# A mixture-of-experts block on one Trainium2 core: w_down products with the tokens as stationary operand in every item, the slots beyond 128 on four column groups

## The reference

```python
logits = h2 @ w_router + b_router            # h2 = rms_norm(x, g_ffn), 32 experts
top_vals, top_idx = top_k(logits, 4)
gates = softmax(top_vals)
for each expert e and each token that chose it:
    a = h2[token] @ w_up[e] + b_up[e]                     # 1024 -> 2048
    hidden = min(a_glu, 7) * sigmoid(1.702 * min(a_glu, 7)) * (clip(a_lin, -7, 7) + 1)
    x[token] += gate * (hidden @ w_down[e] + b_down[e])   # 1024 -> 1024
out = rms_norm(x, g_final)
```

## Time and profile before

| | us |
|---|---|
| median of 3 runs | 2034.45 (2033.26 to 2040.49) |
| the profiled execution, its own time | 2039.02 |
| its span in the trace | 2037.3 |
| TensorE busy in the span | 1969.0 (97%) |
| VectorE, ScalarE, GpSimd busy | 771.6, 653.8, 202.2 |
| mean granted clock of TensorE | 0.983 of full speed |

### The profile page before, as it was taken

The page is one execution under the profiler, slowest core; times in us unless marked ns, Lnnn a source line. Parts: engine busy times, 40 slices in busy tenths (PEclk is TensorE's granted clock), DMA queues, the critical chain, the costliest instruction groups (busy, mean ns, idle before and its releaser), DMA issues.

```text
span 2037.3 us, 38850 instructions
## 1 busy us (share of the span) xinstructions
PE 1969.0 (97%) x14762; PEld 1837.5 (90%) x14762; DVE 771.6 (38%) x1908; ACT 653.8 (32%) x1093; POOL 202.2 (10%) x210
## 2 busy tenths in 40 slices
PE   6999999998699999999999999999999999999997
PEld 5677788877689999999999999999999999999997
DVE  4343277423455445544555442222222222222114
ACT  4222255322155455544555441111111111111113
POOL 0000000001111111111111111111111111110010
PEclk9999899999799999999999999999999999999999
DMA  5223844132799899989998998888888777777774
GB/s 187 79 78 130 255 103 109 55 104 93 260 379 336 310 328 337 332 310 330 339 338 307 332 326 291 287 286 276 288 285 272 269 264 249 259 255 246 259 243 189
DMA packets 241871, 508.02 MB, mean 249 GB/s; under 512 B 13703, under 2 KB 14343, under 8 KB 241792
## 3 DMA queue, kind: packets, MB, share of 16 engines
q1 hardware_dynamic: 224704, 457.91, 63.8%
q0 software_dynamic: 16000, 47.31, 8.2%
q10 hardware_dynamic: 1120, 2.16, 0.3%
HBM read 469.55 MB, written 46.33 MB: 253 GB/s over the span
## 4 chain that ended last, share of the span: by engine, by line
PE 77%; DMA 1%; DVE 1%; issue 1%; ACT 1%; SPq 0%; POOL 0%; DVEq 0%; ACTq 0%; POOLq 0%
PE ps L1839 46%; PE ps L1848 12%; PE ps L1887 3%; PE ps L1889 3%; PE ps L1888 3%; PE ps L1821 2%; PE ps L1730 2%; PE ps L1917 1%; PE ps L1732 1%; PE ps L1731 1%; DMA weights<-in_w_down 1%; PE ps L1754 1%; PE ps L1809 0%; PE ps L1742 0%; PE ps L1893 0%
## 5 line engine op out<-in xcount | busy, mean ns | idle before, releaser
L1839 PE MATMUL ps<-xg,weights 128*128 128x128 f32 (+3 forms) x8192 | 975.8, 281 | 0.7 <-DVE xg L1155 0.7
L1839 PEld LDWEIGHTS ps<-xg,weights 128*128 128x128 f32 x8192 | 968.3, 191 | 2.7 <-issue 1.1
L1848 PE MATMUL ps<-hidden,weights 128*128 128x136 f32 (+2 forms) x2048 | 271.8, 286 | 0.0
L1848 PEld LDWEIGHTS ps<-hidden,weights 128*128 128x128 f32 x2048 | 258.7, 190 | 0.0
L1628 DVE TENSOR_SCALAR glu<-ps,b_up_t 128x128 f32<-128x128 f32 (+3 forms) x256 | 74.1, 351 | 482.4 <-PE ps L1839 482.4
L1349 ACT ACTIVATE glu_sigmoid<-glu 128x512 f32<-128x512 f32 (+3 forms) x64 | 42.1, 658 | 493.2 <-DVE glu L1628 493.2
L1265 POOL DMA_INDIRECT acc_d<-y_rows,row_index_now x62 | 92.4, 1490 | 909.7 <-ACT y_rows L1391 403.0
L1614 DVE TENSOR_TENSOR w_down_rest<-weights,w_down_rest 128x1024 fp32r<-128x1024 f32 x128 | 148.0, 1218 | 31.2 <-ACT w_down_rest L1334 31.2
L1340 ACT ACTIVATE weights_r<-weights 128x1024 fp32r<-128x1024 f32 x128 | 129.5, 1050 | 11.0 <-DVE w_down_rest L1614 7.5
L1334 ACT ACTIVATE w_down_rest<-weights 128x1024 fp32r<-128x1024 f32 x128 | 124.3, 1042 | 11.4 <-DMA weights<-in_w_down 11.4
L1633 DVE TENSOR_SCALAR lin<-ps,b_up_t 128x128 f32<-128x128 f32 (+3 forms) x256 | 74.1, 351 | 114.3 <-PE ps L1839 112.6
(11 more groups left out here) (261 smaller groups left out, 2085.1 us busy)
## 6 DMA issues: line engine op xcount, KB each, us to landing
weights<-in_w_up SPq DMA_DIRECT2D x128, 2048.0 KB, 8.9
weights<-in_w_down SPq DMA_DIRECT2D x64, 2048.0 KB, 10.0
weights<-in_w_in SPq DMA_DIRECT2D x3, 2048.0 KB, 9.4
xt<-in_x SPq DMA_DIRECT2D x8, 512.0 KB, 4.3
qk_d<-stage_rounded SPq DMA_DIRECT2D x16, 256.0 KB, 2.5
qk_d<-stage_rest SPq DMA_DIRECT2D x16, 256.0 KB, 2.8
q_stack<-qk_d SPq DMA_DIRECT2D x16, 256.0 KB
k_stack<-qk_d SPq DMA_DIRECT2D x16, 256.0 KB
```

What stands on the lines that cost most here:

```text
L1839: last = pe.matmul(o, raw[c][:, k, t * P:(t + 1) * P], xg[:, k, 0:w], start=(k == 0), stop=(k == KT - 1))
L1848: last = pe.matmul(o, raw[c][:, k, t * P:(t + 1) * P], hid[:, k, 0:w], start=(k == 0), stop=(k == KT - 1))
```

## The change

What it does:

- `down`, `y_bias`, `y_transposes`, the tiles `y_t` and `b_down_t` and the eight transposes for the latter go. Every item uses `split_down` for its first 128 slots. ScalarE writes the rounded w_down into a tile of its own (`w_down_rounded`), once; VectorE writes the rest over the raw chunk. The products with the rounded weights come first, those with the rest last.
- In items wider than 128, `rest_product` makes the slots 128 to 159 in plain fp32 from the raw chunks: for each k four products with 32 stationary columns of hidden and 256 moving columns of w_down, into the four ranges of 32 partitions of bank 1, and four for the bias. `weight_rest` of these items waits for it (`s_rd`), as it overwrites the raw chunks. ScalarE evacuates that bank in four pieces (`y_rest`).
- The V product of the first token tile is reordered (`first_v_group`), g_mix is loaded as one row and spread by a product with ones, and on VectorE the h rest comes ahead of the weights' rest.
- The forget logits put w_f rounded and its rest side by side (columns 0 to 7 and 32 to 39) in one stationary operand: two products instead of three; the two results are added at the evacuation.
- The router uses banks 6 and 7 in turn; the choice for tile i waits for the one two tiles before. The last root is after the last h_t on ScalarE.
- The gates' sums and scaling go to ScalarE; SP no longer waits for the gathered rows before it loads the first item's chunks 1 to 5.
- At the end acc lies in the buffers of chunks 0 and 1 and the acc rows in chunk 2; the 32 further rows are normed first.

The diff, cut to its core:

```diff
+for half in range(2):
+    act.wait_ge(s_f, half + 1)
+    act.activation(fln[:, half * 512:half * 512 + 512], psum[6 + half][32:32 + NH, :], ACT.Copy).then_inc(s_fa, 1)
 act.wait_ge(s_fv, 3)
 act.activation(fln[:], fabs[:], ACT.Exp, scale=-1.0).then_inc(s_fa, 1)
-act.wait_ge(s_fa, 1)
+act.wait_ge(s_fa, 3)
 act.activation(fln[:], fln[:], ACT.Ln, bias=one[0:NH, :]).then_inc(s_fa, 1)
 def pool_out(g):
             @block.vector
             def _(dve):
-dve.wait_ge(s_c, 32)
+for half in range(2):
+    dve.wait_ge(s_gp, half + 1)
+    dve.tensor_copy(grow[:, half * 512:half * 512 + 512], psum[6 + half][:]).then_inc(s_rs, 1)
...
+def first_v_group(between):
+    tok = slice(0, P)
+    for k in range(KT):
+        if k % 2 == 0:
+            pe.wait_ge(s_va, k // 2 + 1)
+        if k % 4 == 0:
+            pe.wait_ge(s_hl, k // 4 + 1)
+        pe.matmul(psum[0][:], hT_r[:, k, tok], raw_r[HI_SLOT[0]][:, k, :], start=(k == 0), stop=False)
+        pe.matmul(psum[0][:], h_rest[:, k, tok], raw_r[HI_SLOT[0]][:, k, :], start=False, stop=False)
+    between()
+    for k in range(KT):
+        if k % 2 == 0:
+            pe.wait_ge(s_vb, k // 2 + 1)
+        last = pe.matmul(psum[0][:], hT_r[:, k, tok], raw_r[W_SLOT[0]][:, k, :], start=False,
+                         stop=(k == KT - 1))
+    last.then_inc(s_g, 1)
...
 x_transposes(0)
-x_transposes(1)
-for i in range(NT):
+first_v_group(lambda: x_transposes(1))
+x_transposes(2)
+for i in range(1, NT):
...
+    tok = slice(half * 512, half * 512 + 512)
+    for k in range(KT):
+        pe.matmul(psum[6 + half][0:32 + NH, :], wf_r[:, k, :], hT_r[:, k, tok], start=(k == 0), stop=False)
+        last = pe.matmul(psum[6 + half][0:32 + NH, :], wf_r[:, k, :], h_rest[:, k, tok], start=False,
+                         stop=(k == KT - 1))
+    last.then_inc(s_f, 1)
...
-sp.wait_ge(s_gv, 5)
+sp.wait_ge(s_ex, 3)
...
-        sp.wait_ge(s_rw[0], 16)
...
+last = last_item(sp)
 for i in range(NT):
+    if i % 4 == 0:
+        sp.wait_ge(s_pd, last * NCH + (1 + i // 4))
...
+act.wait_ge(s_gv, 1)
+for i in range(NT):
+    last = act.activation(gall[:, i, :], ex[:, i, :], ACT.Copy, accum_out=gsum[:, i, 0:1])
+last.then_inc(s_ex, 1)
...
-def round_copy(i, c):
+def round_weights(i, c):
     act.wait_ge(s_raw[c], 16 * i + 16)
     for q in range(4):
-        act.activation(quarter(wlo[c - 4], q), quarter(raw[c], q), ACT.Copy).then_inc(s_wa, 1)
-def round_chunk(i, c):
-    for q in range(4):
-        act.wait_ge(s_wb, 8 * i + 4 * (c - 4) + q + 1)
-        act.activation(quarter(raw_r[c], q), quarter(raw[c], q), ACT.Copy).then_inc(s_wc, 1)
+        act.activation(quarter(whi[c - 4], q), quarter(raw[c], q), ACT.Copy).then_inc(s_wa, 1)
...
+        round_weights(i, 4 + part)
+        round_hidden(i, part)
+def y_rest(item):
+    act.wait_ge(s_rd, 2 * item + 2)
+    for j in range(4):
+        q = slice(32 * j, 32 * j + 32)
+        last = act.activation(yr[1][0:32, 256 * j:256 * j + 256], psum[1][q, 0:256], ACT.Copy, scale=gc[q, 1:2])
...
+        if c == 1:
+            if w == P:
+                weight_rest(i, 4, range(4))
+            hidden_rest(i, 0)
+        elif c == 2:
+            if w == P:
+                weight_rest(i, 5, range(4))
+        elif w == P:
+            hidden_rest(i, 1)
+        else:
+            for part in range(2):
+                dve.wait_ge(s_rd, 2 * i + part + 1)
+                for down in (4, 5):
+                    weight_rest(i, down, range(2 * part, 2 * part + 2))
+                if part == 0:
+                    hidden_rest(i, 1)
...
-        else:
-            pe.wait_ge(s_rv, RV * (i - 1) + 1)
+        elif i >= 2:
...
+def rest_product(i, part):
+    pe.wait_ge(s_hf, 2 * i + part + 2)
+    for k in range(4 * part, 4 * part + 4):
+        for j in range(4):
+            c, n = 4 + j // 2, 256 * (j % 2)
+            last = pe.matmul(psum[1][32 * j:32 * j + 32, 0:256], hid[:, k, P:], raw[c][:, k, n:n + 256],
+                             start=(k == 0), stop=False)
+    if part == 1:
+        for j in range(4):
+            last = pe.matmul(psum[1][32 * j:32 * j + 32, 0:256], selx[:, 0:32].bitcast(F32),
+                             bdn_r[:, 256 * j:256 * j + 256].bitcast(F32), start=False, stop=True)
+    last.then_inc(s_rd, 1)
+def split_down(i, w, blocks, x_next):
+    for c in (4, 5):
+        pe.wait_ge(s_raw[c], 16 * i + 16)
+    pe.wait_ge(s_bs, i + 1)
     for part in range(2):
-        pe.wait_ge(s_hf, 2 * i + part + 2)
-        for c in (4, 5):
+        if w > P:
             if part == 0:
-                pe.wait_ge(s_evd, 4 * i + c - 1)
-                pe.wait_ge(s_raw[c], 16 * i + 16)
-            for t in (0, 2):
-                if x_next:
-                    x_transpose(pair)
-                    pair += 1
-                products(c, t, part)
-    for c in (4, 5):
-        for t in (1, 3):
-            products(c, t, 0)
-            last = products(c, t, 1)
-            if c == 5 and t == 1:
-                last.then_inc(s_dt, 1)
-        last.then_inc(s_pd, 1)
-def split_down(i, blocks):
-    for part in range(2):
+                pe.wait_ge(s_evd, 4 * i + 3)
+            rest_product(i, part)
         pe.wait_ge(s_ul, 2 * i + part + 1)
         for c in (4, 5):
             if part == 0:
                 pe.wait_ge(s_evd, 4 * i + c - 1)
-                pe.wait_ge(s_raw[c], 16 * i + 16)
-            o, lo = psum[2 * (c % 2)][:], wlo[c - 4]
             for k in range(4 * part, 4 * part + 4):
                 if k % 2 == 0:
-                    pe.wait_ge(s_wc, 8 * i + 4 * (c - 4) + k // 2 + 1)
-                if part == 0:
+                    pe.wait_ge(s_wa, 8 * i + 4 * (c - 4) + k // 2 + 1)
+                if part == 0 and x_next:
                     x_transpose(k + 4 * (c - 4), blocks)
-                hi = raw_r[c][:, k, :]
-                pe.matmul(o, uh[:, k, :], hi, start=(k == 0), stop=False)
-                pe.matmul(o, uh[:, k, :], lo[:, k, :], start=False, stop=False)
-                pe.matmul(o, ul[:, k, :], hi, start=False, stop=False)
-            if part == 1:
-                if c == 4:
-                    pe.wait_ge(s_bs, i + 1)
-                pe.matmul(o, selx[:], bdn_r[:, (c - 4) * CW:(c - 3) * CW], start=False,
-                          stop=True).then_inc(s_pd, 1)
-    pe.sem_inc(s_dt, 1)
+                pe.matmul(psum[2 * (c % 2)][:], uh[:, k, :], whi[c - 4][:, k, :], start=(k == 0), stop=False)
+                pe.matmul(psum[2 * (c % 2)][:], ul[:, k, :], whi[c - 4][:, k, :], start=False, stop=False)
+    for c, part in ((4, 0), (5, 0), (4, 1), (5, 1)) if w > P else ((4, 0), (4, 1), (5, 0), (5, 1)):
+        o = psum[2 * (c % 2)][:]
+        pe.wait_ge(s_wb, 8 * i + (4 * part + 2 * (c - 3) if w > P else 4 * (c - 3)))
+        for k in range(4 * part, 4 * part + 4):
+            pe.matmul(o, uh[:, k, :], raw_r[c][:, k, :], start=False, stop=False)
+        if part == 1:
+            pe.matmul(o, selx[:], bdn_r[:, (c - 4) * CW:(c - 3) * CW], start=False, stop=True).then_inc(s_pd, 1)
+    if w == P:
+        pe.sem_inc(s_rd, 2)
```

More of the change, by code:

```diff
@@ L571, in _ @@
             def _(pe):
-                pe.wait_ge(s_c, 32)
+                pe.wait_ge(s_c, 16)
+                pe.wait_ge(s_eps, 3)
+                for half in range(2):
+                    pe.matmul(psum[6 + half][:], row_of_ones[:], grow[0:1, half * 512:half * 512 + 512],
+                              start=True, stop=True).then_inc(s_gp, 1)
+                pe.wait_ge(s_id, 16)
                 def bank_free(n):
@@ L1055, in build @@
         hid = m.take("hidden", [P, KT, SLOTS], F32)
-        yt = m.take("y_t", [P, KT, SLOTS], F32)
+        gfin = m.take("g_final_row", [P, D], F32)
         wlo_at = m.at
-        wlo = [m.take(f"w_down_rest{i}", [P, KT, CW], F32R) for i in range(2)]
-        ac = [m.take(f"acc{i}", [P, D], F32, at=wlo_at + 4 * D * i) for i in range(NT)]
+        whi = [m.take(f"w_down_rounded{i}", [P, KT, CW], F32R) for i in range(2)]
+        ac = [m.take(f"acc{i}", [P, D], F32, at=raw_at + 4 * D * i) for i in range(NT)]
         uh_at = m.at
@@ L1939, in item @@
                                 x_transpose(k)
[L1940 to L1947 removed]
+                    split_down(i, w, blocks, w < WIDTHS[-1])
                 by_width(pe, ends, item)
```

246 lines of the change are left out of this document (85 added, 161 removed).

## The result

The median of five runs is 2018.47 us (2013.93 to 2022.19), beside 2038.30 for the kernel before in the same comparison (2033.26 to 2045.56): a ratio of 0.990, 95% interval 0.987 to 0.993. The change makes the kernel faster, by 1.0% where 2.2% were forecast (1990 us). The time lies within the stated range, 1976 to 2055, but outside that of the likeliest case, 1976 to 2008. The profiled execution took 2018.47 us, 20.5 less than that of before (2039.02), where the sum said 44 less.

What follows compares the result with a forecast made beforehand. In the item loop only TensorE's own work was taken to count. Terms of -29 -5 -8 -1 -3 -3.7 +5.5 summed to -44 us: profiled execution 1995, median 1990, range 1976 to 2055.

Steps and rivals of the forecast that it cites:

- the likeliest case: Whole kernel: the forecast itself, 44 us less, median 1990 us, range 1976 to 2008; chance 0.50.
- Narrow items, "Nothing": Narrow items' down: same 50 products and transposes, chunk 4 free slightly earlier, next load delayed 1 us; no change in time.
- Wide items, "29 us less": Wide items' down takes 17.4 us: 1.1 us less at width 136, 2.9 less at 152, over 8 and 7 items.
- Rival (a): 32-slot products: strict written order lets a product overlap only one neighbour, 7.8 us an item; 2051 us, slower; chance 0.22.
- Rival (b): 32-slot products: no overlap at all, 11.7 us more for 15 items, some 9 at the end; 2165 us; chance 0.06.
- Rival (d): 32-slot products: overlap real but partial, about 5 us an item; 2008 us; chance 0.12.
- Rival (c): Wide items: VectorE bounds them, 1 to 2 us waited twice an item, 30 us in all; 2020 us; chance 0.06.
- First item, "5 less": First item's down: earlier loads and a single rounding before its first product remove 5.8 us; net 5 less.
- the gather, "1 us" given back: Gather of first rows shares DMA engines with more loads: 1 us lost, bounds 0 to 5.
- Router, "8 less": Router with two banks: seven bank waits of 8.9 us go, less a last choice waiting on the root; bounds 4 and 9.
- Start, "3 less": Start: g_mix as one row and first V products needing only rounded weights save 3 us; bounds 0 and 6.
- End, "5.5 more": End: VectorE held by the last item's weight rests delays the acc scalings, 5.5 us more; bounds 2 and 9.

Runs made afterwards that it cites:

- either cure: Changed kernel with half of chunk 5's rest behind the second hidden rest, or with a k's three products together again in narrow items: narrow period 41.440 or 41.426 us.
- an edit had them back: Changed kernel with wide items' last products chunk by chunk and half of narrow items' chunk 5 rest moved later: wide periods 48.040 and 51.453, median 1997.28 us.
- the edit at the end: Acc squares and scalings moved inside the last item, on the changed kernel with two loop edits: 1998.76 us ahead of the hidden rounding, 1994.44 with squares behind it.

## Why the prediction was right or wrong

*Right in sign, more than twice too large.* The sum said 44 us less, the profiled executions differ by 20.5. The time falls outside the likeliest case (1976 to 2008) and inside the full range, which was made wide by rivals whose mechanisms did not come. Of the 23.5 us by which the sum missed, 10.5 lie in the narrow items and 13.3 in the wide ones; elsewhere more and less cancel. That they cancel is luck: start and router gained 5.9 us more than forecast, attention and the stretch behind the router took 4.6 more. Two steps failed: the narrow items' term, put at nothing, by its mechanism, and the wide items' term by its size.

*Narrow items, "Nothing": wrong, 10.5 us.* This step had no mechanism for what came. It counted the products ("same 50 products and transposes") and looked at when buffers come free, but not at their order: the products with the weights' rest went behind the second hidden half, and with them 8 x 0.22 us of the cover that VectorE had. The rows for it were at hand: 8 steps of 0.80 us, 6.4, became 8 of 0.58, 4.6 (4.8 measured), against a VectorE with four quarters of rests, 4.6 us, in its queue ahead of lin. The slack was worked out for the wide items, where the 32-slot products add cover, and taken as good for the narrow ones, where there is none. The experiments give the term: 0.67 us an item in the mean of 15, gone by either cure, and item 15, whose cover is longer, has none of it.

*Wide items, "29 us less": the mechanism right, the size wrong; 15.8.* Removing `down` gives what the rows said, and the 50 products with their transposes take 13.7 us (13.5 forecast). The four column groups work side by side, 4.15 us for 3.9 forecast: one after another they were put at 15.6, so the factor is 3.8. Some 0.1 us stands at the item's end. The down part is so 0.6 us longer than forecast, 9 us in 15 items, and the next item's first groups take 0.26 longer, 4 us more. Of the 13.3 us, 5.5 (8 x 0.35 + 7 x 0.39) are the alternating last products, and an edit had them back. The rest, 7.8 us or 0.52 an item, is about what the four changes between 128 and 32 columns cost, 0.6 by the estimate above. The prediction said that such a change costs nothing, from the y transposes, where it cannot be told from the rest of their 0.12 us. I had also asked who is late inside the item, and not when the result's banks come free for the next one.

*Rival (a), strict order,* is refuted by the records: groups start 7 ns apart although each product has two. The Trainium skill's "TensorE: Matmul & The Clock Gate" (The mechanism) says that matmuls start and end strictly in program order; the traces here disagree for products on different column groups, for records of the bias products start before records of products written ahead of them, and 1.87 us per 32 records leaves no room for strict order. The order of the stream matters all the same, 4.59 us when it is unkind. *Rival (b)* did not come either (its terms add up to 2175, not 2165). *Rival (d)* had 5 us an item and a total nearer to the measured one (2008), but for a reason that did not come: the overlap is almost whole. *Rival (c)* was near: with the slot products away VectorE is the bound. With them the wait for its hidden rest appeared in the narrow items and in the last one, not in the 15 of rival (c).

*First item, "5 less", and the gather, "1 us" given back.* The first item's part came close in size (5.1 for the 5.8 of the working). Of its two reasons one is shown, the early loads: without them the item is 2.6 us longer than before (51.9 and 49.3) in spite of the single rounding. The early loads made TensorE's wait for the gather 2.9 us longer (9.5, and 6.6 when they are held back), within its bounds of 0 to 5, three times the value taken.

*Router, "8 less":* 11.8, of which the bank is 9.3; the wait rows had 8.9. The deduction of 0.5 us for the last choice did not show, and 2.4 us beside the banks were not forecast.

*Gates, "1 less":* the stretch from table product to index product is 1.0 us shorter, and 0.6 us was lost ahead of it.

*Start, "3 less":* 5.1 (bounds 0 to 6): 3.0 by the order, and 2.1 left for g_mix, which the sum had not parted. *Forget logits, "3.7 less"*: 3.7. *End, "5.5 more"*: 5.8, with its mechanism: VectorE is free for the first scaling at 1993.06, 13.0 us after the last group (13.2 forecast).

*Attention:* 2.1 us more, with no edit there, and in the experiments' profiles from 5.0 us less to 6.6 us more than in the changed kernel's. Why is open; nothing was tried on it.

## What to carry to other kernels

When products are regrouped, count the work that stands ahead of each wait again, for every class of item; the same work in another order can leave TensorE waiting for a producer that was hidden before. After each group ask also when its banks come free for the next one: finish one bank's sum before the other's last products. Do not put work that waits for a load in front of a short step on which TensorE depends; in front the edit at the end gained 0.7 us, behind it (and with six of the eight scalings) 6.4. When a wait appears, look at the granted clock behind it as well: in the version without the slots it cost 0.9 us an item on top of 2.1.

## What the runs showed of the hardware

- fp32 products with 32 stationary and 256 moving columns on four column groups, alternating between the groups: 32 records in 1.87 us, 0.058 each, where one such record is 0.216; a factor of 3.7. Records of other groups start ahead of one whose group is busy, also ahead of the written order.
- This reaches only over a few records: with eight records in a row on one group, the same 32 take 4.59 us, a factor of 1.5.
- Four changes between 128 and 32 stationary columns an item cost about 0.6 us, 0.15 each: an estimate from the starts and pieces of one item (72 records 4.15 us for 3.89, the pieces behind them 0.15 and 0.20 us longer).
- Behind an idle stretch of 2.0 to 2.2 us an item the granted clock fell to the lower of its two levels (1.2 and 2.4 GHz) in nine of 15 wide items: products of 512 columns started 0.43 us apart in place of 0.23, and an item of width 136 took 48.31 us in place of 46.74. Behind idle stretches of the same length it held in the other six.
- A table load on ScalarE took 1.28 us.
- TensorE waited 2.9 us longer for the gather of the first rows with five more 2 MB loads beside it (9.5 and 6.6 us).
